# Layer 1's feed-forward norm in two parts of 128 tokens, with the next product's first two slots taken together, and three reorderings around it

## The reference, cut to what matters

```python
x = x + gt1 * m_lat                       # m_lat = mixer output @ w_out
x = x + gt2 * conv_ffn(modulate(rms_norm(x, norm_ffn_g[i]), sh2, sc2),
                       ffn_up[i], ffn_conv[i], ffn_down[i])
# after layer 0 the same for y_ctx; layer 1 gives only the 256 latent tokens
# rms_norm(x, g) = x * rsqrt(mean(x * x) + eps) * g ; modulate(h, b, s) = h * (1 + s) + b
```

## Time and profile before

| what | value |
|---|---|
| median of 3 runs | 1557.83 us |
| the profiled execution | 1556.83 us |
| its span, first to last instruction | 1555.0 us |
| TensorE matmul busy | 1429.3 us, 92% of the span |
| TensorE weight load busy | 1195.6 us, 77% |
| VectorE busy | 888.4 us, 57% |
| ScalarE busy | 599.6 us, 39% |
| GpSimd busy | 142.2 us, 9% |
| granted TensorE clock, mean | 0.965 |

### The profile page before, as it was taken

One profiled execution on the slowest core, in us unless ns is written; L12 is line 12 of the kernel. 1 busy time (PEld: TensorE's weight loads), 2 busy tenths in 40 slices (PEclk: granted clock), 3 DMA queues, 4 the chain that ended last, 5 costly groups with the idle time before them and its releaser, 6 DMA issues. The chain is left out here.

```text
span 1555.0 us, 30846 instructions
## 1 busy us (share of the span) xinstructions
PE 1429.3 (92%) x13547; PEld 1195.6 (77%) x13547; DVE 888.4 (57%) x1268; ACT 599.6 (39%) x968; POOL 142.2 (9%) x153
## 2 busy tenths in 40 slices
PE   3798999898999799999999999999999998799998
PEld 2566676777887688777778888877877768799998
DVE  3558643544464445655555223779685665688844
ACT  2333534221231244333334113453553453455534
POOL 1000000233242020000000001100002330000000
PEclk8999989799999899999999999999999999899999
DMA  9321101143315131665562323213242003366643
GB/s 326 85 81 54 55 29 39 57 159 117 112 60 163 56 109 40 187 180 163 163 189 81 108 82 115 69 54 109 82 124 93 2 3 142 111 181 189 190 163 109
DMA packets 169744, 172.30 MB, mean 111 GB/s; under 512 B 15270, under 2 KB 135946, under 8 KB 169610
## 3 DMA queue, kind: packets, MB, share of 16 engines
q1 hardware_dynamic: 167216, 165.14, 35.1%
q0 software_dynamic: 1088, 4.19, 0.7%
q10 hardware_dynamic: 1306, 0.99, 0.2%
HBM read 169.26 MB, written 1.05 MB: 110 GB/s over the span
## 5 line engine op out<-in xcount | busy, mean ns | idle before, releaser
L310 DVE TENSOR_TENSOR w_lo<-w_raw,w_hi 128x2048 fp32r<-128x2048 f32 x95 | 216.1, 2275 | 229.2 <-ACT w_hi L300 229.1
L635 PE MATMUL bank<-h,w_hi 128*128 128x256 f32 (+2 forms) x968 | 333.4, 344 | 8.5 <-issue 5.9
L638 PE MATMUL bank<-h,w_hi 128*128 128x256 f32 (+2 forms) x968 | 324.5, 335 | 0.0
L639 PE MATMUL bank<-h,w_lo 128*128 128x256 f32 (+2 forms) x968 | 324.4, 335 | 0.0
L300 ACT ACTIVATE w_hi<-w_raw 128x2048 fp32r<-128x2048 f32 x95 | 180.4, 1900 | 206.7 <-PE bank L635 160.0
L653 DVE SCALAR_TENSOR_TENSOR acc<-bank,params,acc 128x510 f32<-128x510 f32 (+3 forms) x272 | 173.1, 646 | 84.1 <-ACT acc L1639 63.4
L635 PEld LDWEIGHTS bank<-h,w_hi 128*128 128x128 f32 (+1 forms) x968 | 185.1, 191 | 43.6 <-issue 25.2
L638 PEld LDWEIGHTS bank<-h,w_hi 128*128 128x128 f32 (+1 forms) x968 | 185.2, 191 | 20.3 <-issue 2.9
L639 PEld LDWEIGHTS bank<-h,w_lo 128*128 128x128 f32 (+1 forms) x968 | 184.9, 191 | 18.9
L1639 ACT ACTIVATE acc<-bank,params 128x512 f32<-128x512 f32 (+1 forms) x88 | 48.6, 580 | 155.8 <-PE bank L639 55.8
L635 PE MATMUL bank<-h_hi,w_hi_hyb 128*128 128x512 f32 (+1 forms) x184 | 77.2, 420 | 12.6 <-DVE h_lo L609 4.4
(11 more groups left out here) (416 smaller groups left out, 2843.5 us busy)
## 6 DMA issues: line engine op xcount, KB each, us to landing
w_raw<-in_ffn_up SPq DMA_DIRECT2D x88, 512.0 KB, 5.3
w_raw<-in_mod_w SPq DMA_DIRECT2D x40, 1024.0 KB, 5.3
w_raw<-in_ffn_down SPq DMA_DIRECT2D x22, 1024.0 KB, 4.9
w_raw<-in_ssm_w_in SPq DMA_DIRECT2D x20, 1024.0 KB, 5.3
w_raw<-in_hyb_w_in SPq DMA_DIRECT2D x9, 1024.0 KB, 5.3
w_raw<-in_ssm_w_out SPq DMA_DIRECT2D x8, 1024.0 KB, 4.9
mod_early<-in_mod_w SPq DMA_DIRECT2D x4, 1024.0 KB, 17.8
mod_early<-in_mod_w POOLq DMA_DIRECT2D x4, 1024.0 KB, 14.9
```

The source lines that it names most:

```text
L310: dve.tensor_tensor(lo, raw, hi.bitcast(F32), ALU.subtract).then_inc(k.lo_done.sem, 1)
L635: mm = pe.matmul(out, wh, xh, start=(start and n == 0), stop=False)
L638: pe.matmul(out, wh, xl, start=False, stop=False)
L639: mm = pe.matmul(out, wl, xh, start=False, stop=(stop and n == last))
```

## The change

- Layer 1 gets `PartNorm` in place of `Norm` (which is deleted), with `parts=2` on its row product: two parts of 128 tokens. `FfnUp` gets `paired=True`, so that its first two slots are taken together in `pe_first_slots`, and a GpSimd block is added.
- In all three places with extra slots (layer 0's output projection, its feed-forward's down projection, and now layer 1's output projection) the two extra slots stand ahead of the last slot of the row product: in the load order, in ScalarE's splits and in VectorE's.
- In `SsmIn`, turns 0 to 6 are moved one chunk later (0 after chunk 6, 1 after 7, 2 and 3 after 8, 4 after 9, 5 and 6 after 10), and ScalarE's tok j stands in the round after the chunk that its turn follows.

```diff
-def row_loads(k, w, n_slots):
+def row_loads(k, w, n_slots, extra=()):
     r = w.rearrange("(s k p) n -> s p k n", k=2, p=P)
-    first = len(k.stream.plan)
+    slots = []
     for s in range(n_slots):
-        k.stream.add("split", [("rows", None, r[s])])
-    return first
+        ahead = [k.stream.add("extra", parts) for parts in extra] if s == n_slots - 1 else None
+        slots.append(k.stream.add("split", [("rows", None, r[s])]))
+    return slots, ahead
...
+    def turns(self, i):
+        return {6: (0,), 7: (1,), 8: (2, 3), 9: (4,), 10: (5, 6)}.get(i, (i - 4,) if 10 < i < self.n_tok + 4 else ())
...
-            for j in {4: (), 5: (0,), 6: (1,), 7: (2, 3)}.get(i, (i - 4,)):
-                if j < self.n_tok:
-                    turn(j)
+            for j in self.turns(i):
+                turn(j)
...
-            j = self.feat(i - 4)
-            if j is not None and j < self.n_tok:
+            for j in self.turns(i - 1):
                 tok(j)
...
 (layer 0, ScalarE; VectorE in the same way)
-            row0.act_splits(act, 2, 4)
+            row0.act_splits(act, 2, 3)
             extra_hi(k, act, g_up[0])
             extra_hi(k, act, g_up[1])
+            row0.act_splits(act, 3, 4)
...
-            down.act_splits(act, 1, KF // 2)
-            extra_hi(k, act, g_ssm)
-            extra_hi(k, act, g_ssm + 1)
+            down.act_splits(act, 1, KF // 2 - 1)
+            extra_hi(k, act, g_ssm[0])
+            extra_hi(k, act, g_ssm[1])
+            down.act_splits(act, KF // 2 - 1, KF // 2)
...
 (layer 1)
-        row1 = RowGemm(k, 1, 2, g_sout, SI // P // 2, ..., LC, opens=True, ynorm=ynorm)
-        norm = Norm(k, 1, 1, row1, h[0], h[1], b)
-        up = FfnUp(k, 1, g_up, g_down, norm, gh, gl, b.acc)
+        row1 = RowGemm(k, 1, 2, g_sout, SI // P // 2, ..., LC, opens=True, ynorm=ynorm, parts=2)
+        norm = PartNorm(k, 1, 1, row1, h[0], h[1], b, g_up)
+        up = FfnUp(k, 1, g_up, g_down[0], norm, gh, gl, b.acc, paired=True)
...
-            row1.pe(pe)
-            norm.pe(pe)
+            row1.pe(pe, after=norm.pe_after)
...
                 ynorm.act_hi(act, c)
-                if c % 2 == 1:
+                if c % 2 == 1 and c < 15:
+                    if c == 13:
+                        extra_hi(k, act, g_up[0])
+                        extra_hi(k, act, g_up[1])
                     row1.act_splits(act, c // 2 + 1, c // 2 + 2)
...
+        @block.gpsimd
+        def _(pool):
+            norm.pool(pool)
...
-                if c >= 2 and c % 2 == 0:
+                if c >= 2 and c % 2 == 0 and c < 16:
+                    if c == 14:
+                        extra_lo(k, dve, g_up[0])
+                        extra_lo(k, dve, g_up[1])
                     row1.dve_splits(dve, c // 2, c // 2 + 1)
```

More of the change, by code:

```diff
@@ L199, in hyb_loads, with col_loads, up_parts, pair_loads @@
     return first
-def col_loads(k, w, c0, c1, width=2 * P, kind="split"):
+def col_loads(k, w, c0, c1, width=2 * P):
     r = w.rearrange("(k p) n -> p k n", p=P)
-    first = len(k.stream.plan)
-    for c in range(c0, c1, width):
-        k.stream.add(kind, [((0, width), r[:, :, c:c + width])])
-    return first
-def pair_loads(k, w, mod=None, g0=0, extra=False):
+    return [k.stream.add("split", [((0, width), r[:, :, c:c + width])]) for c in range(c0, c1, width)]
+def up_parts(r, c):
+    return [((0, P), r[:, :, c * P:c * P + P]), ((P, P), r[:, :, F + c * P:F + c * P + P])]
+def pair_loads(k, w, mod=None, g0=0, first=()):
     r = w.rearrange("(k p) n -> p k n", p=P)
@@ L214, in pair_loads @@
     for c in range(KF):
+        if c < len(first):
+            slots.append(first[c])
+            continue
         slots.append(len(k.stream.plan))
-        k.stream.add("extra" if extra and c < 2 else "split",
-                     [((0, P), r[:, :, c * P:c * P + P]), ((P, P), r[:, :, F + c * P:F + c * P + P])])
+        k.stream.add("split", up_parts(r, c))
         if mod is not None and 2 <= c < 18:
@@ L223, in pair_loads, with att_row_loads @@
     return slots
-def row_loads(k, w, n_slots):
+def row_loads(k, w, n_slots, extra=()):
     r = w.rearrange("(s k p) n -> s p k n", k=2, p=P)
-    first = len(k.stream.plan)
+    slots = []
     for s in range(n_slots):
-        k.stream.add("split", [("rows", None, r[s])])
-    return first
-def att_row_loads(k, w):
-    first = len(k.stream.plan)
+        ahead = [k.stream.add("extra", parts) for parts in extra] if s == n_slots - 1 else None
+        slots.append(k.stream.add("split", [("rows", None, r[s])]))
+    return slots, ahead
+def att_row_loads(k, w, extra):
+    slots = []
     for a in range(2):
@@ L242, in att_row_loads @@
             parts.append(("rows", par, w[r0:r0 + P, :].rearrange("(k p) n -> p k n", p=HD)))
-        k.stream.add("split", parts)
+        slots.append(k.stream.add("split", parts))
     r = w.rearrange("(s k p) n -> s p k n", k=2, p=P)
-    for s in range(2, 4):
-        k.stream.add("split", [("rows", None, r[s])])
-    return first
+    slots.append(k.stream.add("split", [("rows", None, r[2])]))
+    ahead = [k.stream.add("extra", parts) for parts in extra]
+    slots.append(k.stream.add("split", [("rows", None, r[3])]))
+    return slots, ahead
 def mod_loads(k, w, g0, g1):
@@ L1142, in pe @@
         for s in range(self.n_slots):
-            ns = k.stream.plan[self.g0 + s][1]
+            ns = k.stream.plan[self.g[s]][1]
             pe.wait_ge(k.hi_done.sem, ns + 1)
@@ L2497, in pe @@
                 continue
-            n = k.stream.plan[self.g0 + s][1]
+            n = k.stream.plan[self.g[s]][1]
             if m == 0:
```

162 lines of the change are left out of this document (35 added, 127 removed).

## The result

The changed kernel takes 1600.34 us (median of 4 runs, 1596.05 to 1607.57) beside 1558.63 us for the kernel before (4 runs): ratio 1.0269, 95% interval 1.0241 to 1.0296. It is slower by 42 us, where 13 were forecast. The sign, the stage and most terms were right; one term, the 288 narrow matmuls of layer 1, came out at nearly twice its size.

The account below looks back on a forecast made before the run. TensorE's time line was taken as the bound (matmuls busy 92%). Terms -5.6 - 3.8 + 5 + 17.7 = +13.3 us on 1556.83 gave 1570.1, median 1571; likeliest range 1563 to 1580, 8 in 10 from 1556 to 1590.

Parts of the forecast that it names:

- 288 x 0.111: Layer 1's halves: 144 matmuls at 0.120 (17.3 us) become 288 of 128 columns at 0.111 (32.0 us), plus 14.7 us.
- 24 matmuls at 0.213 and 72 at 0.111: Layer 1's slot 7 after its pause: slow start, then full clock, 13.1 us where it was 5.8: +7.3.
- the first two slots: Layer 1's next product: 192 x 0.111 plus sums, spread and a wait, 22.7 us where it was 14.8: +7.9.
- Rival (c): Layer 1: narrow float32r matmuls go as plain f32, two passes of 0.111, 32 us more, 1603; chance 0.13.
- The range of 0.067 to 0.222: Bounds in us for one 128-column float32r matmul in layer 1: only columns count, or two records of 0.111.
- Rival (a): Layer 1: weight loads don't bind, narrow matmuls go at 0.067, 12.7 us less, 1558; chance 0.10.
- Slot 7 comes late: Layer 1: its load waits behind the extra slots, TensorE stands 8.5 us, slot 7 starts 8.2 us later (6 to 10).
- rival (d): Layer 1: slot 7's load is hidden, 8 us and a slow start less, 1561; chance 0.10.
- The norm's hole: Layer 1's 9.7 us hole becomes 0.8 us of sums and spread and a 1.2 us wait for h: -7.7.
- The split of slot 4: Behind layer 1's first two slots, this split stands behind the taps of slot 2: +2 us (0 to 3.5).
- Layer 0: Reordered splits let sums come sooner: -5.6 us behind the output projection, -3.8 us behind the down projection.
- The turns: SSD projection: moved turns wait for token copies, 3.0, 3.5, 1.5 and 1.9 us: +5 (bounds -6 and +8).

Follow-up runs that it names:

- e3: Kernel before, four warm mid-stream slots of layer 1's up product split into halves of 128 columns (384 float32r matmuls): 1580.57 us beside 1560.24.
- e9: Changed kernel with 64 unread 256-column matmuls filling TensorE's 8 us pause ahead of layer 1's slot 7: 1588.05 us, ratio 1.0169 to the kernel before.
- e12: Changed kernel with both the 8 us pause and the 1.2 us wait for the first h filled by unread matmuls: 1569.89 us, ratio 1.0068 to before.
- e7: Kernel before, four slots of layer 1's up product in 128-column halves with only 64 weight columns: 1552.94 us beside 1559.60.
- e6: Changed kernel with layer 1's slot 7 loaded and split ahead of the two extra slots, as before the change: 1594.32 us, ratio 1.0215 to before.
- e14: Changed kernel, pause kept, with layer 1's 288 narrow matmuls reading plain f32, two records each: 1603.85 us beside the changed kernel's 1600.
- e2: Changed kernel with layer 1, turns and copies put back, so only layer 0's splits are reordered: 1551.13 us, ratio 0.9935 to the kernel before.
- e5: Kernel before with only the new places of the turns and their copies: 1565.22 us, ratio 1.0024 to the kernel before.
- e1: Changed kernel with layer 1 put back; layer 0's reordered splits and the new turns stay: 1556.99 us, ratio 0.9985 to the kernel before.
- e10: Kernel before with layer 0's splits reordered and 51 unread matmuls in the hole of layer 1's old norm: 1548.93 us, ratio 0.9934 to before.
- e13: Kernel before with layer 0's splits reordered, old turns, and ScalarE's first three token copies one round later: 1550.86 us, ratio 0.9933 to before.
- e4: Kernel before, four warm slots of layer 1's up product in 128-column halves read as plain f32: 1619.94 us, +60.

## Why the prediction was right or wrong

**The size of a narrow matmul.** The term "288 x 0.111" is the one that failed, not by its distance but by the step ahead of it. For slot 7 I wrote "24 matmuls at 0.213 and 72 at 0.111", and I gave the first two slots the full clock throughout: I took the 5 us of slow start of the earlier trace rows, which are those of a 256-column stream, and put them on a 128-column one. The distance itself was right: 0.112 at full clock in e3, e9 and e12. The weight load sets it (e7). The 264 matmuls that I had put at full clock ran at the low one: 264 x (0.2135 - 0.111) = 27.1 us of the 30.0 by which that row is off. Most of the rest is sums and spreads, which took the low clock too: the stretch is 67.9 us, of which 61.5 are the 288 matmuls and 1.2 the wait for h, so they took some 5 us where 2 were forecast.

**What holds the clock down.** Shown: this stream keeps a high clock (e3, 43 us) and didn't raise a low one (after, 65 us; e6, 57 us; e9, 41 us). The 8 us pause lowers it, in e9 a wait of 1.2 us inside such a stream was enough too, and with both filled it stays up (e12). Also shown: the same products as plain f32 raise it and keep it over the same wait (e14). In the 256-column streams of the same traces waits of 0.4 us at every slot of the row product cost nothing. Longer waits ahead of a 256-column stream lower the clock in some executions and not in others: the wait of 2.0 us in layer 1's down product does in the trace of before and does not in that of after.

```profile
1486.98 0.55 PE L635 MATMUL bank<-ffn_g_hi,w_hi 128*128 128x256 f32 x1 [2.00 <-issue]
1487.33 0.42 PE L638 MATMUL bank<-ffn_g_lo,w_hi 128*128 128x256 f32 x1
...
1530.23 0.36 PE L640 MATMUL bank<-ffn_g_hi,w_hi 128*128 128x256 f32 x1 [1.97 <-issue]
1530.42 0.28 PE L643 MATMUL bank<-ffn_g_lo,w_hi 128*128 128x256 f32 x1
```

The first two rows are of before (the granted clock of 1487 to 1492 is 0.66), the last two of after (1.00). Not shown: why the two kinds of stream differ, and from which width on a float32r stream raises the clock; between 128 and 256 nothing was tried.

**Rival (c)** gave 1603 and the measurement is 1600, for another reason. It says two passes at full clock; the clock read 0.50, and a warm matmul takes one pass of 0.11. The range of 0.067 to 0.222 had the size inside; its weight was too small, since the upper bound lies near the low clock's distance, 0.213, which the earlier trace rows show. That rival (c) came within 3 us is luck: two passes at full clock and one at half of it cost nearly the same. Rival (a) falls: no stream here with 128 weight columns ran below 0.111. The rule of the Trainium skill weighed in the prediction ("TensorE: Matmul & The Clock Gate", Back-to-back issue gap, about 81 ns) doesn't hold here: the traces show 0.111 warm with 128 weight columns and 0.060 with 64.

**Slot 7 comes late.** Right, step by step. Its load is issued at 1326.39 (predicted 1330.6 in the time of before, which this trace runs 4.3 us ahead of here), ScalarE splits it at 1331.12, VectorE at 1333.13, and the pause is 8.02 us for 8.5. Its price was read too low: it also set the clock for what came behind. That the slow start would last wasn't in the sum, nor in rival (d), which gave the pause 8 us "and a slow start".

**The norm's hole and the first slots.** The wait for the first h is 1.16 (1.2 forecast). The sums and spreads sit inside the stream, but at the low clock. The split of slot 4 (+2 forecast, 0 to 3.5) cost nothing: from 1404.79 on TensorE has no wait but the 2.0 us that the trace of before has too. The +0.8 of the last row is made of something else: the first 24 matmuls behind 1404.79 are still at the low clock (+2.3), and the fall shown above, at 1486.98, is missing in this trace (-1.5).

**Layer 0.** Right. With the 2.0 us by which this execution is ahead, the sums come at 574.9 (574.9 forecast), the first h at 581.4 (580.8), the product goes on at 584.4 (584.2): -5.4 for -5.6. The second norm gives -3.5 for -3.8. e2 gives 9 to 10 us together by its runs.

**The turns.** Right in sign and place: four waits of 2.56, 1.87, 1.44 and 1.87 us for 3.0, 3.5, 1.5 and 1.9. The second was overestimated, so +3.3 for +5. e5 gives 3.7 by the ratio, e2 against e1 8, each with an interval some 3 to 5 us wide on either side; the thirteen traces give 3.3.

**Not in the sum.** The +3.3 us of the SSD stage. 1.5 of it lies behind the 2.9 us wait at 1122.78 and ahead of the first decay product, 1.8 in the short pause at the head of the out product (6.05 us from the root's spread to the first product, for 4.27 before, e1 and e2). Both are falls of the clock: behind that wait the granted clock of 1123 to 1127 is 0.57 where before has 1.00, and in the pause it is 0.50 for 1.00. Of the fourteen traces seven have the first (after, e5, e6, e10, e12, e13, e14) and seven the second. Executions of the same code differ: e10 has both and e2 neither, and e9 has only the second, though up to slot 7 its code is that of the changed kernel. So they come and go by chance between executions. None of the four traces with the code of before up to there has either (before, e3, e4, e7); whether the reorderings make such falls likelier, and so cost more than the waits they add, stays open. With it -2.0 at the start, the two nearly cancel by chance.

**As a whole.** Layer 1's halves cost 31 us by the clock (after against e12) and 13 us by the late slot 7 and the doubled weight loads, less the hole that they close (e12 against e1); layer 0's reorder gives 9 to 10 back (e2), the turns take 4 (e5) to 8 (e1 against e2). The parts come to 38 with the smaller figure and to 42 with the larger. The version to keep is e2: 0.65% faster than the kernel before, 3.3% faster than the changed one.

## What to carry to other kernels

Cutting a product into narrower moving tiles to open an earlier start has two prices: the weight loads per column double, and the stream may lose its power to bring the clock back after a pause. So look at what stands ahead of the narrow stretch and inside it: here waits of 8.0, 3.8 and 1.2 us each nearly doubled the time of all that came behind. A slow start seen behind one kind of stream is not to be lent to another: read the granted clock for that kind, or put both distances in as cases. And where a split is moved ahead of a slot, the room must come from slack of that stage: slots of 512 columns had it, those of 256 had none.

## What the runs showed of the hardware

- Float32r matmuls with 128 moved columns on 128 weight columns start 0.111 to 0.112 us apart at a granted clock of 1.00 and 0.213 at 0.50; on 64 weight columns 0.060 at 1.00. At 256 columns it is 0.120 at 1.00 and 0.213 at 0.50: at the low clock the narrow one takes as long as one with twice the columns.
- A stream of them ran 43 us at full clock (e3), and 65 us at the lower level without rising (after). The plain f32 stream rose within 6 us, and kept 1.00 over a wait of 1.16 us (e14).
- The clock fell 1.3 us behind the end of a wait of 1.19 us in the narrow stream (e9); with ten 256-column matmuls in that wait it didn't (e12).
- The same wait of 2.9 us ahead of a 256-column stream was followed by a fall of the clock in seven of fourteen traces, and cost 1.5 us there.
- Filling the two waits with products that nobody reads was worth 31 us here (after against e12), though the filler computes nothing that is used.
